# Seven block products in place of eight in half of a down projection, and one tap of a convolution moved to ScalarE

## The reference

```python
def conv_gated_ffn(x, w_up, conv_w, conv_b, w_down):
    gu = x @ w_up                                   # 2048 -> 2 * 5632
    gate, up = gu[..., :D_FF], gu[..., D_FF:]
    gate = causal_depthwise_conv(gate, conv_w, conv_b)   # 3 taps along the tokens, plus a bias
    return (jax.nn.silu(gate) * up) @ w_down        # 5632 -> 2048

h = h + conv_gated_ffn(rms_norm(h, norm_ffn_g[i]), ...)
```

## Time and profile before

| | |
|---|---|
| median of 3 runs | 2181.2 us (2180.76 to 2181.27) |
| span of the profiled execution | 2179.3 us |
| TensorE busy | 2168.1 us, 99% |
| TensorE weight loads | 1881.8 us, 86% |
| VectorE busy | 1500.1 us, 69% |
| ScalarE busy | 1046.6 us, 48% |
| DMA, mean rate | 187 GB/s |

### The profile page before, as it was taken

How to read it: one execution, slowest core, us unless ns; L and a number is a source line. 1 busy time by engine, 2 the same in 40 slices (tenths; PEclk the granted TensorE clock), 3 DMA queues, 4 the chain that set the end, 5 groups by cost and what they waited for, 6 DMA issues and landing times.

```text
span 2179.3 us, 32163 instructions
## 1 busy us (share of the span) xinstructions
PE 2168.1 (99%) x11646; PEld 1881.8 (86%) x11646; DVE 1500.1 (69%) x1919; ACT 1046.6 (48%) x1339; POOL 45.3 (2%) x110
## 2 busy tenths in 40 slices
PE   9999999999999999999999999999999999999998
PEld 8898888888888888888898988888888888888886
DVE  6797567676677766676557975767766677766764
ACT  6555544444444444445554654444444444443554
POOL 2000000000000000000000000000000000000011
PEclk9999999999999999999999999999999999999999
DMA  8645565555655555555556455555555555555562
GB/s 265 213 136 175 185 203 188 187 187 183 202 192 186 194 178 192 192 175 200 181 180 181 136 186 189 191 193 192 192 174 191 193 195 190 192 191 187 179 213 97
DMA packets 233292, 406.45 MB, mean 187 GB/s; under 512 B 14828, under 2 KB 50268, under 8 KB 233096
## 3 DMA queue, kind: packets, MB, share of 16 engines
q1 hardware_dynamic: 231976, 402.72, 55.9%
q0 software_dynamic: 512, 1.76, 0.3%
q10 hardware_dynamic: 736, 1.07, 0.1%
HBM read 403.42 MB, written 2.10 MB: 186 GB/s over the span
## 4 chain that ended last, share of the span: by engine, by line
PE 99%; issue 0%; ACT 0%; POOL 0%; DVE 0%; POOLq 0%; ACTq 0%
PE acc L1887 16%; PE tps L1887 16%; PE acc L1706 12%; PE acc L1708 12%; PE acc L1707 12%; PE tps L1897 8%; PE acc L1897 8%; PE tps L1707 4%; PE tps L1708 4%; PE tps L1706 4%; PE tps L1763 1%; PE acc L1793 1%; PE tps L2062 0%; PE tps L1697 0%; PE tps L2036 0%
## 5 line engine op out<-in xcount | busy, mean ns | idle before, releaser
L1107 DVE TENSOR_TENSOR w_lo<-raw,w_hi 128x1024 fp32r<-128x1024 f32 (+1 forms) x768 | 920.2, 1217 | 444.2 <-ACT w_hi L934 309.1
L934 ACT ACTIVATE w_hi<-raw 128x1024 fp32r<-128x1024 f32 x508 | 529.4, 1059 | 664.4 <-PE acc L1887 129.7
L1887 PE MATMUL acc<-xa,w_hi 128*128 128x512 f32 x1536 | 366.0, 391 | 0.0
L1887 PE MATMUL tps<-xa,w_hi 128*128 128x512 f32 x1536 | 361.2, 390 | 0.0
L663 ACT ACTIVATE w_hi<-raw 128x1024 fp32r<-128x1024 f32 (+1 forms) x259 | 261.2, 1041 | 154.7 <-PE acc L1708 127.1
L1887 PEld LDWEIGHTS tps<-xa,w_hi 128*128 128x128 f32 x1536 | 285.3, 188 | 57.2
L1887 PEld LDWEIGHTS acc<-xa,w_hi 128*128 128x128 f32 x1536 | 283.7, 188 | 56.2 <-DVE h L1444 0.4
L1706 PE MATMUL acc<-w_hi,xb_hi 128*128 128x512 f32 x560 | 220.5, 394 | 0.0
L1708 PE MATMUL acc<-w_lo,xb_hi 128*128 128x512 f32 x560 | 218.1, 389 | 0.0
L1707 PE MATMUL acc<-w_hi,xb_lo 128*128 128x512 f32 x560 | 217.9, 389 | 0.0
L1897 PEld LDWEIGHTS acc<-xa,w_lo 128*128 128x128 f32 x1536 | 192.7, 191 | 5.1
(11 more groups left out here) (235 smaller groups left out, 2308.6 us busy)
## 6 DMA issues: line engine op xcount, KB each, us to landing
raw<-in_w_up SPq DMA_DIRECT2D x176, 1024.0 KB, 4.9
raw<-in_w_down SPq DMA_DIRECT2D x88, 1024.0 KB, 4.9
raw<-in_w_out SPq DMA_DIRECT2D x32, 1024.0 KB, 5.0
raw<-in_w_ple_gate SPq DMA_DIRECT2D x32, 1024.0 KB, 4.9
raw<-in_w_in SPq DMA_DIRECT2D x21, 1024.0 KB, 5.3
raw<-in_w_ukv SPq DMA_DIRECT2D x8, 1024.0 KB, 5.5
raw<-in_w_in SPq DMA_DIRECT2D x8, 864.0 KB, 4.7
raw<-in_w_uq SPq DMA_DIRECT2D x6, 1024.0 KB, 5.5
```

What stands on the lines that cost most here:

```text
L934: copy(w_hi[:, half_of(m), :], raw[:, c % RAW_SLOTS, (m % 2) * HALF:(m % 2 + 1) * HALF], ACT.Copy).then_inc(hi_done, 1)
L1107: dve.tensor_tensor(w_lo[:, half_of(m), 0:n], raw[:, c % RAW_SLOTS, at:at + n], w_hi[:, half_of(m), 0:n].bitcast(F32), ALU.subtract).then_ ...
L1887: ins = pe.matmul(dst, hi[:, k * BLK + n * P:k * BLK + (n + 1) * P], x_both[:, kt, :, :].rearrange("p a s -> p (a s)"), start=kt == 0, sto ...
```

## The change

In the loop, for column blocks 0 and 1 together, the eight block products of 128 tokens x 256 features x 512 columns (tokens in 2 parts, features in 2, columns in 2) become seven products of sums (Winograd's form of Strassen's scheme). The sums of activations S1 to S4 are formed by VectorE in `up_f` and split into a free part of `xb`; the sums of weights T1 to T4 are formed by VectorE in place in `raw` (`t_sum`) and split once more from there, so a pass has 27 halves where it had 24. Three of the seven products go straight into `h`, four into a new tile `corner_sum`, which is set to zero once per layer by GpSimd and folded into `h` after the loop (`fold`). The slots of the two corner chunks are given back only when T4 has been split. 27 is odd, and the six slots of `w_hi` need an even count, so a pass of the loop now has two units.

The bias and last tap go to ScalarE (`tap_2`). The second product with the token factors (L1544) is left out of the unit; the factor is applied as `h` is added (`by_token`).

The core of the diff, without the renumbering of halves, blocks and jobs:

```diff
-ACC_UNIT = 4
-JOB_UNIT = 8
+ACC_UNIT = 6
+JOB_UNIT = 12
+TURN_UNITS = 2
+CORNERS = 7
...
+    UNIT_HALVES = 2 * UNIT_CHUNKS + CORNERS - 4
...
+        FORM_B11, FORM_B21, FORM_B22, FORM_T1, FORM_T3, FORM_T2, FORM_T4 = range(2 * 2 * (KT // 4), 2 * 2 * (KT // 4) + CORNERS)
+        PLAIN = FORM_T4 + 1
...
+                    freed = (-(UNIT_HALVES - 1 - FORM_T4),) * 2 + (-2, 0) if n < RAW_SLOTS else [2 * (n - RAW_SLOTS) + 2]
...
+                pool.memset(corner_sum[:, :, :], 0.0).then_inc(corners_zero, 1)
...
+                def tap_2(l, u):
+                    act.wait_ge(gate_step, 3 * UNITS * l + 3 * u + 3)
+                    for ft in range(4):
+                        copy(conv[:, ft, :], gate_f[:, ft, :], ACT.Identity,
+                             bias=prm[:, bass.ds(4 * u + (BIAS + ft), 1)],
+                             scale=prm[:, bass.ds(4 * u + (TAP[2] + ft), 1)]).then_inc(conv_step, 1)
...
+                    go(2, 7)
+                    act.wait_ge(s_step, made(l, w, i, 4))
+                    copy(s_hi.rearrange("p c k s -> p (c k s)"), up_f[:, :, :].rearrange("p a s -> p (a s)"),
+                         ACT.Copy).then_inc(s_split_hi, 1)
+                    go(7, 9)
                     for k in range(2):
+                        halves_used(act, l, m0 + 7, w)
                         copy(gate_f[:, 2 * k:2 * k + 2, :], acc[k][:, :, S:2 * S], ACT.Copy).then_inc(gate_lo, 1)
+                    go(9, 11)
+                    tap_2(l, u)
+                    go(11, 13)
                     act.wait_ge(conv_done, UNITS * l + u + 1)
                     copy(gate_f[:, :, :], conv[:, :, :], ACT.Tanh, scale=0.5).then_inc(tanh_done, 1)
...
+                def by_token(dst, src, t):
+                    return dve.scalar_tensor_tensor(dst, src, rstd["ffn"][:, t:t + 1], dst, ALU.mult, ALU.add)
...
+                    go(2, 4)
+                    s_sums(w, i, 0)
+                    s_sums(w, i, 1)
+                    go(4, 5)
+                    s_sums(w, i, 2)
+                    go(5, 6)
+                    s_sums(w, i, 3)
...
+                    go(10, 12)
+                    tap_1(u)
+                    go(12, 13)
+                    tap_0(u)
+                    t_sum(w, i, 1, corner(i, 0, 0), corner(i, 1, 0), corner(i, 0, 0))
+                    go(13, 15)
+                    t_sum(w, i, 2, corner(i, 1, 0), corner(i, 1, 1), corner(i, 1, 0))
+                    silu(u)
+                    t_sum(w, i, 3, corner(i, 1, 1), corner(i, 1, 1), corner(i, 0, 0))
+                    go(15, 16)
+                    t_sum(w, i, 4, corner(i, 0, 1), corner(i, 0, 1), corner(i, 1, 1))
+                    go(16, 17)
+                    gated(u)
+                    go(17, 19)
+                    dve.wait_ge(corners_zero, l + 1)
+                    product_added(FORM_B11, corner_sum[:, 0], acc[0][:, 0, :], None, acc_free[0])
+                    product_added(FORM_B21, h_block(0, 0), acc[0][:, 1, :], 0, acc_free[0])
+                    go(19, 21)
+                    product_added(FORM_B22, h_block(0, 1), acc[1][:, 0, :], 0, acc_free[1])
+                    product_added(FORM_T1, corner_sum[:, 1], acc[1][:, 1, :], None, acc_free[1], 3)
...
+                    p1, p5, p7, p6 = (corner_sum[:, k] for k in range(4))
...
+                    if j == 0:
+                        dve.tensor_tensor(p6, p6, p1, ALU.add).then_inc(corner_folded, 1)
+                        by_token(h[:, 0, 0:BLK], p1, 0).then_inc(corner_folded, 1)
+                        dve.wait_ge(corner_folded, done + 2)
+                        dve.tensor_tensor(p1, p6, p7, ALU.add).then_inc(corner_folded, 1)
+                        dve.wait_ge(corner_folded, done + 3)
+                        by_token(h[:, 1, 0:BLK], p1, 1).then_inc(corner_folded, 1)
                     else:
+                        dve.tensor_tensor(p6, p6, p5, ALU.add).then_inc(corner_folded, 1)
+                        dve.tensor_tensor(p1, p1, p5, ALU.add).then_inc(corner_folded, 1)
+                        dve.wait_ge(corner_folded, done + 2)
+                        by_token(h[:, 0, BLK:2 * BLK], p6, 0).then_inc(corner_folded, 1)
+                        by_token(h[:, 1, BLK:2 * BLK], p1, 1).then_inc(corner_folded, 1)
...
                 for j in range(N_BLK):
-                    add_block(l, bd + j, j, None, True)
+                    fold(l, j)
+                    add_block(l, bd + j, j)
...
+                def corner_product(m, w, a, dst):
+
+                    hi, lo = halves(l, m, w)
+                    for k in range(2):
+                        cols = slice(k * BLK, (k + 1) * BLK)
+                        ins = three(dst, a[0][:, k], a[1][:, k], hi[:, cols], lo[:, cols], k == 0, k == 1)
+                    ins.then_inc(w_used, 1)
...
+                    corner_product(m0 + FORM_B11, w, a11, acc[0][:, 0, :])
+                    corner_product(m0 + FORM_B21, w, a12, acc[0][:, 1, :])
+                    pe.wait_ge(s_split_lo, (UNITS - 1) * l + u)
+                    free_acc(l, b0 + 3, w)
+                    corner_product(m0 + FORM_B22, w, s4, acc[1][:, 0, :])
+                    corner_product(m0 + FORM_T1, w, s1, acc[1][:, 1, :])
+                    for n, a in ((0, s3), (1, s2), (2, a22)):
+                        corner_product(m0 + FORM_T3 + n, w, a, new_job(l, j0 + 4 + n, w))
+                    for _ in down(m0 + PLAIN, b0 + 4, gt, w):
+                        pass
+                    for _ in down(m0 + PLAIN + 2, None, gt, w, j0 + 7):
+                        pass
```

More of the change, by code:

```diff
@@ L98, in layer_plan @@
         last[block["poolw"] + i] = 2 * chunk["poolw"] + i
-    for name, ends in (("out", (11, 15, 23, 31)), ("ffn", (7, 7, 23, 23, 33, 35)),
+    for name, ends in (("out", (11, 15, 23, 31)), ("ffn", (7, 7)),
                        ("ple", (1, 1, 9, 17, 19, 19, 27, 35))):
         for i, m in enumerate(ends):
-            last[block[name] + i] = 2 * chunk[name] + m
+            last[block[name] + i] = 2 * chunk[name] + m + (extra if name == "ple" else 0)
     for i in range(n_blk):
-        last[block["ple"] - n_blk + i] = 2 * (chunk["ple"] - n_blk + i) + 1
-    return dict(last=last, n_blk=n_blk, units=units, kt=kt, chunk=chunk, chunks=c, block=block, blocks=b, job=job, jobs=j)
+        last[block["ple"] - n_blk + i] = 2 * (chunk["ple"] - n_blk + i) + 1 + extra
+    return dict(last=last, extra=extra, n_blk=n_blk, units=units, kt=kt, chunk=chunk, chunks=c, block=block, blocks=b, job=job, jobs=j)
 def head_jobs(first):
@@ L970, in _ @@
+                first_unit(l)
+                with act.Fori(0, LOOPS) as w:
+                    for i in range(TURN_UNITS):
+                        unit(l, w, i)
                 act.wait_ge(g_done, UNITS * l + UNITS)
                 copy(xa[0][:, 0:4, :], conv[:, :, :], ACT.Copy).then_inc(g_hi, 1)
-                d0 = 2 * (CHUNKS - plan["n_blk"] * 4 - 2 - N_BLK)
+                d0 = M_DOWN
                 def ple_job(j):
@@ L1578, in _ @@
-                unit(l, 0, 0, False)
-                with dve.Fori(1, UNITS) as u:
-                    unit(l, u, u - 1, True)
-                d0 = 2 * (CHUNKS - 4 * N_BLK - 2 - N_BLK)
+                    steps(l, m0 + 2, m0 + 4)
+                    rows_spread()
+                    steps(l, m0 + 4, m0 + 8)
+                    rows_kept()
+                    steps(l, m0 + 8, m0 + 9)
+                    dve.wait_ge(rows_done, l + 1)
+                    gate_sum(0, 0)
+                    gate_sum(0, 1)
@@ L2179, in unit @@
-                    by_rows(m0 + 8, up_bank, 0, 8, v)
-                    if with_down:
-                        pe.wait_ge(g_lo, UNITS * l + u)
-                        for j in range(N_BLK):
-                            for _ in down(m0 + 16 + 2 * j, b0 + 2 + j, gt, v,
-                                          None if j < 2 else j0 + 4 + 2 * (j - 2)):
-                                pass
-                jobs_split(l, JB["ffn_norm"] + 5)
-                unit(0, 0, False)
-                with pe.Fori(1, UNITS) as u:
-                    unit(u, u - 1, True)
@@ L2193, in _ @@
+                jobs_split(l, JB["ffn_norm"] + 5)
+                first_unit()
+                with pe.Fori(0, LOOPS) as w:
+                    for i in range(TURN_UNITS):
+                        unit(w, i)
+                m, b = M_DOWN, BL["ple"] - N_BLK
                 pe.wait_ge(g_lo, UNITS * l + UNITS)
```

471 lines of the change are left out of this document (288 added, 183 removed).

## The result

The changed kernel takes 2191.73 us (median of four executions, 2190.89 to 2193.76) against 2181.0 us for the kernel before (median of four as well): a ratio of 1.005, 95% interval 1.0038 to 1.0062. It is slower by 10.7 us where 2.6 us less was forecast; the time lies inside the range given. The profiled execution has a span of 2192.0 us, 12.7 more than before.

A forecast was written before the change was run, and what follows sets the result against it. TensorE, busy 99% of the span, was taken as the bound. Matmuls -27.2, loop losses +15.2 and folds +9.4 gave -2.6 on 2179.3, or 2176.7; with 1.9 for launch and end, 2178.6 us, range 2163 to 2193.

The forecast's parts named there:

- the price of the taps on ScalarE: Loop, ScalarE: the four taps ahead of half 15's split take 1.57 us, at most 0.35 more.
- The moved tap neither costs nor gains: Loop: ScalarE has half 15 ready at T = 30.46, VectorE began it at 30.53, so nothing is lost.
- A taps' row much over 0.4 us each: ScalarE's taps in the trace: a row this long was named as a sign that the prediction is wrong.
- The chain from T = 38: Per loop unit (T = 0 at its gate rows) VectorE never waits from 38.11; half 23 comes late, TensorE loses 0.76 us.
- rival (c): Products' stage: VectorE's thirteen long operations cost their full 1.22 us, loss 1.8 per unit, 2199 us (at half, 2189); chance 0.18.
- just in time: Products' stage: halves 21 and 22 arrive at T = 50.97 and 52.11 for weight loads due at 51.02 and 52.38.
- the point: Loop: TensorE's loss per unit above which the change loses, put at 0.89 us.
- The loads: Loop: two corner loads of 1 MB start at T = 52.1 and land by 61.9; TensorE wants half 27 at 65.5: hidden.
- Rival (d): TensorE's longer loop code no longer stays on the engine; each of 2 x 4 branches waits: 13.6 us, 2192; chance 0.10.
- The folds: Behind the loop: TensorE loses 1.95 and 2.75 us to VectorE's two folds, 4.7 per layer, 9.4 in all.

## Why the prediction was wrong, point by point

**The step that failed: the price of the taps on ScalarE.** The prediction took "the nearest row, four scaled copies of 256 columns in 1.57 us", with "four single ones of 0.48, 0.35 more" as the bound above. They take 2.07: 0.49 from start to start and 0.588 each, where the copies take 0.36 and 0.46 to 0.48. The real price lay outside the bound (1.57 + 0.35 = 1.92). The copy has one pointer operand, for the scale, and reads PSUM; the tap has a second one, for the bias, and reads SBUF. No run parts the two. "The moved tap neither costs nor gains" became 0.50 us at half 15, which the chain of waits (tap, tanh, half 17) carried whole to half 23. Twenty units of it are 10 of the 13 us between 2178.6 and 2191.7, and putting the taps back gave 9.1 us; the other 3 are the tail behind the loop, below. "A taps' row much over 0.4 us each" was the prediction's own sign of being wrong.

The Trainium skill has a price for this: "ScalarE: Activation LUTs", section "What ACT_TABLE_LOAD costs", gives 186 ns plus 0.833 ns a column plus about 93 ns for each pointer operand, with back-to-back ones overlapping by 93 ns. An estimate from that page is 585 ns for one tap and 492 between two. The trace agrees: 588 and 493 ns.

**The chain from T = 38: right.** 15.15 us to half 23 for 15.12; the weight sums come 1.14 apart, so rival (c)'s 1.22 was not paid, and with the assumed start the loss is 0.75 for 0.76. What was wrong in it nearly cancelled: TensorE's matmul followed VectorE's end by 0.13, not 0.28, and the matmul behind a restart comes 0.11 late. Halves 21 and 22 were forecast "just in time": with the late start half 21 opens a gap of its own, which only takes from the later one, as was said.

So (c)'s outcome came (a loss above 0.89 per unit) by another mechanism: not longer operations, a later start. With the tail as measured in the median, 10.7 + 27.2 - 25.4 = 12.5, the point is lower, (27.2 - 12.5)/20 = 0.74, and the run with the taps back, which loses 0.75, is even with the kernel before to 1.5 us.

**The loads, and the branch: right.** No wait of TensorE ends at a DMA, and the units follow each other at 66.11 to 66.13 whether or not a branch lies between. Between 500 and 900 us, with at least three branches back, no packet of instructions came. Rival (d) is refuted by this and by the run without weight sums. The prediction weighed two sentences of the Trainium skill, page "Runtime: NRT & Kernel Launch", section "Instruction fetch mechanics". Room for 2048 instructions agrees with the trace, in which a body of two units, 2 x (347 + 346) = 1386 matmuls and loads, is repeated without a gap at its branch. Two lines of 256 do not agree with it for TensorE; the page counts them for 32 KiB, and gives TensorE 128 KiB.

**The folds: right in size (1.86 and 2.77 for 1.95 and 2.75), incomplete.** Put at nothing without a reason were the wait before `p_tok`'s transposes (0.74 and 0.79) and the clock (about 0.4 a layer in a median execution, 1.3 to 1.6 where it fell). Both follow from VectorE's lateness one step on: late at the end of the loop, it met GpSimd's subtraction; late with the second fold, it let TensorE stand for 3 us.

**Where it could have been better.** The rows already showed idle time on VectorE where an operation without a deadline could stand: 2.07 us ahead of half 17, of which the first weight sum takes only 1.14. A forecast of an order of work should ask of each operation not only what it costs but whether it can go into the last gap in front of the chain.

## What to carry to other kernels

When an engine has room on average and a stage without room, what counts is when the stage's unbroken chain starts and what stands in it that could stand elsewhere: here the same work in another order turned a kernel that was 0.5% slower than the one before into one that is 1.0% faster. Price an operation by a row of its own form, with the same operands from the same memories, before moving it in front of something that a chain waits for. When a fix reveals less than it should, look for the next limit close behind, as the half slot behind the taps.

## What the runs showed of the hardware that was not expected

VectorE's subtraction of two SBUF tiles does not run beside GpSimd's: the first of the two splits took 2.12 of the 3.25 us, and ended 1.08 us behind the end of GpSimd's operation (962.18 + 2.60 = 964.78), about where it would have ended if it had started there; with that operation left out both took 2.35. VectorE's adds from PSUM during it kept their time (two in 1.41; 1.40 without). The Trainium skill, "SBUF — State Buffer", section "SBUF: two separate sides", says that the port pair the two share is an exclusive lock, and that a VectorE operation with two SBUF inputs needs it while GpSimd reads SBUF; the trace agrees.

TensorE was granted 1.2 GHz after standing for 3.0 us in the middle of a stretch at 2.4 GHz, in some executions and not in others. This goes with a scatter of the executions: they lie 2.9 us apart in the changed kernel, 0.7 with the first fold only and 0.5 without the folds. The mean granted clock of each execution moves with its time: without GpSimd's subtraction it is 0.999 at 2188.82 us, 0.998 at 2190.13 to 2190.22 and 0.997 at 2191.37.
